# Two score maps of a differential attention head: from zero-padded 128-row operands to shared 64-row halves

## The reference

```
p1 = softmax(q1 @ k1.T * scale - slope * |t - s|)
p2 = softmax(q2 @ k2.T * scale - slope * |t - s|)
o  = (p1 - lam * p2) @ v        # then RMS norm over 128, gain
```

## Time and profile before

| what | value |
|---|---|
| median of 3 runs | 916.52 us |
| the runs | 917.79, 916.52, 912.07 us |
| span of the profiled execution | 912.4 us |
| busy in it: PE, PEld, DVE, ACT, POOL | 83%, 70%, 66%, 57%, 28% |

### The profile page before, as it was taken

One profiled execution on the slowest core, in us unless ns is written; L12 is line 12 of the kernel. 1 busy time (PEld: TensorE's weight loads), 2 busy tenths in 40 slices (PEclk: granted clock), 3 DMA queues, 4 the chain that ended last, 5 costly groups with the idle time before them and its releaser, 6 DMA issues. The chain is left out here.

```text
span 912.4 us, 13783 instructions
## 1 busy us (share of the span) xinstructions
PE 754.5 (83%) x4074; PEld 638.1 (70%) x4074; DVE 602.4 (66%) x1003; ACT 518.5 (57%) x960; POOL 257.5 (28%) x309
## 2 busy tenths in 40 slices
PE   3999999978887988779995249999999999999810
PEld 3998899867675766658884237888877777777600
DVE  6831210498885777731655954989988888888525
ACT  2252321778885888731125004878887787877412
POOL 5010000154453444320124461232123322232116
PEclk9999999989997999969995559999999999999965
DMA  8122110000002000039133722999999999999543
GB/s 301 62 57 82 49 55 1 1 21 2 1 1 92 1 2 0 1 93 372 69 137 117 253 93 60 362 389 365 388 391 388 378 377 388 391 389 381 184 156 143
DMA packets 70986, 159.50 MB, mean 175 GB/s; under 512 B 7457, under 2 KB 15649, under 8 KB 70945
## 3 DMA queue, kind: packets, MB, share of 16 engines
q1 hardware_dynamic: 66048, 141.16, 41.3%
q0 software_dynamic: 4896, 17.83, 7.6%
HBM read 139.57 MB, written 19.40 MB: 174 GB/s over the span
## 5 line engine op out<-in xcount | busy, mean ns | idle before, releaser
L1917 DVE TENSOR_TENSOR eDl<-rawD,eDh 128x1024 fp32r<-128x1024 f32 x64 | 75.4, 1219 | 14.0 <-ACT eDh L1861 13.8
L1917 DVE TENSOR_TENSOR eGl<-rawG,eGh 128x1024 fp32r<-128x1024 f32 x64 | 76.2, 1222 | 11.8 <-ACT eGh L1861 10.9
L1917 DVE TENSOR_TENSOR eUl<-rawU,eUh 128x1024 fp32r<-128x1024 f32 x64 | 75.0, 1221 | 4.9 <-ACT eUh L1861 4.3
L1976 POOL DMA_INDIRECT acc_rows<-yg,idx_s x17 | 27.3, 1605 | 157.8 <-ACT yg L1886 157.8
L1861 ACT ACTIVATE eGh<-rawG 128x1024 fp32r<-128x1024 f32 x64 | 66.1, 1057 | 5.8 <-DMA rawG<-in_w_gate 4.7
L1861 ACT ACTIVATE eUh<-rawU 128x1024 fp32r<-128x1024 f32 x64 | 63.5, 1053 | 7.2 <-DMA rawU<-in_w_up 7.2
L1809 PE MATMUL bank<-eGh,xgT_h 128*128 128x512 f32 x136 | 56.8, 418 | 12.4 <-DVE xgT_l L1922 11.8
L1861 ACT ACTIVATE eDh<-rawD 128x1024 fp32r<-128x1024 f32 x64 | 64.0, 1055 | 0.0
L480 DVE TENSOR_TENSOR w_l<-w_raw,w_h 128x1024 fp32r<-128x1024 f32 (+2 forms) x16 | 17.7, 1146 | 66.3 <-ACT w_h L379 66.3
L312 PE MATMUL bank<-w_h,xT_h 128*128 128x256 f32 (+1 forms) x192 | 55.1, 287 | 2.8 <-DVE xT_l L472 2.8
L1830 PE MATMUL bank<-eDh,hT_h 128*128 128x512 f32 x136 | 53.8, 395 | 2.2 <-DVE hT_l L1934 2.2
(11 more groups left out here) (325 smaller groups left out, 2366.8 us busy)
## 6 DMA issues: line engine op xcount, KB each, us to landing
rawG<-in_w_gate SPq DMA_DIRECT2D x68, 512.0 KB, 14.2
rawU<-in_w_up SPq DMA_DIRECT2D x68, 512.0 KB, 11.3
rawD<-in_w_down SPq DMA_DIRECT2D x68, 512.0 KB, 11.0
w_raw<-in_w_in SPq DMA_DIRECT2D x7, 1024.0 KB, 5.8
wo_raw<-in_w_o SPq DMA_DIRECT2D x16, 256.0 KB, 4.9
acc_rows<-ax SPq DMA_DIRECT2D x7, 512.0 KB, 2.6
x_rows<-res SPq DMA_DIRECT2D x6, 512.0 KB, 2.8
res<-acc_rows SPq DMA_DIRECT2D x6, 512.0 KB, 5.7
```

The costliest lines, as they stand in the source:

```text
L1917: nc.vector.tensor_tensor(wl_[X][i][:], raw_of(X, t, i)[:], f32(wh_[X][i][:]), ALU.subtract).then_inc(s_lo[X], 1)
L1976: pool.indirect_dma_start(out=acc_rows, out_offset=bass.IndirectOffsetOnAxis(ap=idx_s[:, 0:1], axis=0), in_=yg[:], in_offset=None, bounds_ ...
```

## The change

The queries of both maps go into one tile per sequence, laid out as the keys are. ACT and DVE cut them with one 128-partition instruction where there were two of 64. The zero rows, their memsets and their semaphore `s_zero` are gone. PE takes 64 partitions of q and k for each matmul: 0 to 63 for map 0 and 64 to 127 for map 1. The six matmuls of a tile now alternate between the maps, so that map 0's sum is complete after the fifth and map 1's after the sixth, where it was the third and the sixth. PE's wait for the two free banks of a tile is now one wait, for both, ahead of the first matmul. `s_qkh` counts 4 per head instead of 6, `s_ql` 2 instead of 4.

```diff
-    q_h = [[at(f"q_h{x}{m}", 78 + 6 * m + 4 * x, [P, SEQS[x][1]], FR) for m in range(2)] for x in range(2)]
-    q_l = [[at(f"q_l{x}{m}", 80 + 6 * m + 3 * x, [P, SEQS[x][1]], FR) for m in range(2)] for x in range(2)]
+    q_h = [at(f"q_h{x}", 78 + 4 * x, [P, SEQS[x][1]], FR) for x in range(2)]
+    q_l = [at(f"q_l{x}", 80 + 3 * x, [P, SEQS[x][1]], FR) for x in range(2)]
...
                 if qt == 0:
 
-                    wait(pe, s_zero, 2 * x + 2)
-                    wait(pe, s_ql, 4 * h + 2 * x + 2)
+                    wait(pe, s_ql, 2 * h + x + 1)
                     wait(pe, s_kl, 2 * h + x + 1)
-                for m in range(2):
-
-                    wait(pe, s_bias, 2 * g - 4 + m + 1)
-                    qs = slice(qt * P, (qt + 1) * P)
-                    out = psum[2 * (i % 2) + m][:, 0:n]
-                    nc.tensor.matmul(out, q_h[x][m][:, qs], kk_h[x][:], start=True, stop=False)
-                    nc.tensor.matmul(out, q_l[x][m][:, qs], kk_h[x][:], start=False, stop=False)
-                    nc.tensor.matmul(out, q_h[x][m][:, qs], kk_l[x][:], start=False, stop=True).then_inc(s_sc, 1)
+                wait(pe, s_bias, 2 * g - 4 + 2)
+                qs = slice(qt * P, (qt + 1) * P)
+                last = []
+                for k, (q, kk) in enumerate(((q_h, kk_h), (q_l, kk_h), (q_h, kk_l))):
+                    for m in range(2):
+                        r = slice(64 * m, 64 * m + 64)
+                        last.append(nc.tensor.matmul(psum[2 * (i % 2) + m][:, 0:n], q[x][r, qs], kk[x][r, :],
+                                                     start=(k == 0), stop=(k == 2)))
+                last[-2].then_inc(s_sc, 1)
+                last[-1].then_inc(s_sc, 1)
...
-                for m in range(2):
-                    r = slice(64 * m, 64 * m + 64)
-                    nc.scalar.activation(q_h[x][m][r, :], dqT[r, h, t0:t0 + n], ACT.Copy).then_inc(s_qkh, 1)
+                nc.scalar.activation(q_h[x][:], dqT[:, h, t0:t0 + n], ACT.Copy).then_inc(s_qkh, 1)
...
-            for x in range(2):
-                for m in range(2):
-                    r = slice(64 - 64 * m, 128 - 64 * m)
-                    nc.gpsimd.memset(f32(q_h[x][m][r, :]), 0.0)
-                    nc.gpsimd.memset(f32(q_l[x][m][r, :]), 0.0).then_inc(s_zero, 1)
...
-            pool.wait_ge(s_zero, 4)
             stage(0, 0)
...
-                for m in range(2):
-                    r = slice(64 * m, 64 * m + 64)
-                    wait(dve, s_qkh, 6 * h + 3 * x + m + 2)
-                    nc.vector.tensor_tensor(q_l[x][m][r, :], dqT[r, h, t0:t0 + n], f32(q_h[x][m][r, :]), ALU.subtract).then_inc(s_ql, 1)
+                wait(dve, s_qkh, 4 * h + 2 * x + 2)
+                nc.vector.tensor_tensor(q_l[x][:], dqT[:, h, t0:t0 + n], f32(q_h[x][:]), ALU.subtract).then_inc(s_ql, 1)
```

More of the change, by code:

```diff
@@ L585, in encoder_trunk @@
     s_alibi = sem("alibi_landed")
-    s_zero = sem("zero_rows_ready")
     s_qkh, s_ql, s_kl = sem("diff_qk_high"), sem("diff_q_low"), sem("diff_k_low")
@@ L906, in cut_q @@
                 t0, n, _ = SEQS[x]
-                for m in range(2):
-                    r = slice(64 * m, 64 * m + 64)
-                    wait(dve, s_qkh, 6 * h + 3 * x + m + 2)
-                    nc.vector.tensor_tensor(q_l[x][m][r, :], dqT[r, h, t0:t0 + n], f32(q_h[x][m][r, :]), ALU.subtract).then_inc(s_ql, 1)
+                wait(dve, s_qkh, 4 * h + 2 * x + 2)
+                nc.vector.tensor_tensor(q_l[x][:], dqT[:, h, t0:t0 + n], f32(q_h[x][:]), ALU.subtract).then_inc(s_ql, 1)
             def cut_k(h, x):
                 t0, n, _ = SEQS[x]
-                wait(dve, s_qkh, 6 * h + 3 * x + 1)
+                wait(dve, s_qkh, 4 * h + 2 * x + 1)
                 nc.vector.tensor_tensor(kk_l[x][:], dkT[:, h, t0:t0 + n], f32(kk_h[x][:]), ALU.subtract).then_inc(s_kl, 1)
```

## The result

The changed kernel takes **927.1 us** in the median of four runs (919.5 to 930.5), the kernel before 914.3 (908.3 to 917.8) on the same chip: a ratio of **1.0135, with a 95% interval of 1.0075 to 1.0195**. The forecast was 907.6 us; the time lies outside its range, on the other side of no change, and within 0.4 us of the 927.5 that one rival gave, the one in which the clock falls. I had given it 0.04. The intervals in this document are worked out from the runs that lie within 1.5% of the quickest of their kernel, which for every kernel but e10 are all of them.

A forecast was written before the change was run, and what follows sets the result against it. The differential block was taken as one chain along DVE, crossing to ACT at six waits, with PE slack. Savings 5.8 + 2.2 + 0.9 = 8.9 us from a 916.5 us median gave 907.6 us, range 903 to 914.5.

The forecast's parts named there:

- Parts 1 and 2: Cuts of q for heads 1 to 3: one instruction instead of two saves 5.8 us on DVE, 2.2 us through ACT.
- Part 3: Block start: first bias instruction comes sooner, gaining 0.9 us, between -0.2 (maps' matmuls in turn) and 1.8 (side by side).
- The sum: Whole change: cuts on DVE, cuts on ACT and block start, 5.8 + 2.2 + 0.9 = 8.9 us saved.
- Part 4: PE's score matmuls in the heads: 7 us or 3.5 us a head, both covered by PE's slack, so 0 gained.
- The rival of the clock: Differential block: less PE work brings more low-clock stretches; half the stage low costs +11 us, 927.5 us; chance 0.04.
- The array empties at each switch: PE's scores: each switch between halves makes a matmul cost 0.39 us, not 0.23; +10 us, 926.5 us; chance 0.07.
- The low ends: Cuts and start: POOL slows the surviving cut, ACT's relief becomes waits, start gains nothing; 4.1 us saved, 912.4 us; chance 0.22.
- Concurrent maps also shorten the heads: Scores in the heads: six matmuls take the time of three, saving 10.7 us in all, 905.8 us; chance 0.17.

The follow-up runs named there:

- e10: Changed kernel plus two 64-row filler matmuls (rows 0 to 63) ahead of each tile's scores; ten runs from 904.9 to 940.3 us, median 923.5.
- e2: Changed kernel, but each score matmul takes all 128 rows, so each bank sums both maps; 904.43 us, 0.9899 of the kernel before.
- e6: Changed kernel with three full-row score matmuls per tile instead of six on 64 rows, other products left out; 960.64 us, total not comparable (more expert tiles).
- e1: Changed kernel, but map 0's three 64-row score matmuls are issued before map 1's three; 924.35 us, 1.0119 of the kernel before.
- e5: Changed kernel, but both maps' score matmuls use rows 0 to 63, map 1's scores left out; 971.39 us, total not comparable (more expert tiles).
- e3: Changed kernel plus two full-row filler matmuls ahead of each tile's six scores, into banks the scores overwrite; 906.11 us, 0.9926 of the kernel before.
- e4: Kernel before with only the scores changed: 64 rows, alternating maps, one wait for both banks; 931.11 us, 1.0175 of the kernel before.
- e7: Changed kernel plus one full-row filler matmul ahead of each tile's six scores; 907.08 us, 0.9940 of the kernel before.
- e8: Changed kernel plus four full-row filler matmuls ahead of each tile's six scores; 915.73 us, 1.0014 of the kernel before.
- e9: Changed kernel plus full-row filler matmuls, one ahead of each long-sequence tile and four ahead of each short one; 901.67 us, 0.9869 of the kernel before.
- e12: Changed kernel plus four full-row filler matmuls ahead of each short-sequence tile, none ahead of long ones; 902.00 us, 0.9881 of the kernel before.

## Why the prediction was wrong

**Parts 1 and 2, the cuts, held.** In the changed kernel DVE cuts q once per sequence, in 0.69 and 0.42 us, so none of the surviving cuts inside the heads was slowed, though POOL's `second` runs beside each of them:

```profile
208.98 0.42 DVE L899 TENSOR_TENSOR q_l<-dqT,q_h 128x256 fp32r<-128x256 f32 x1
...
218.96 0.69 DVE L899 TENSOR_TENSOR q_l<-dqT,q_h 128x512 fp32r<-128x512 f32 x1
```

In e2, where PE does not disturb it, head 2 takes 19.62 us, head 1 18.92; the forecast said about 20.5. So these two heads gave 3.5 and 3.7 us instead of 2.6 each, and head 0 gave less (0.6), for a sum over the three of 7.8 us against the 8.0 of Parts 1 and 2.

**Part 3, the start, held in kind.** The scores of the two halves ran beside each other, the case that I had priced at 1.8 us:

```profile
183.07 0.83 DVE L899 TENSOR_TENSOR q_l<-dqT,q_h 128x512 fp32r<-128x512 f32 x1
...
185.78 0.69 DVE L926 CUSTOM_DVE_ANT_0 ee<-bank,bias_t 128x512 f32<-128x512 f32 x1 [0.32 <-PE bank L744]
```

The first bias instruction comes 1.6 us sooner than in the earlier trace rows. Beside the staging copies that moved to where the memsets were, the first cut of q takes 0.83 us and the key cut ahead of it 0.83 (0.69 before), the few tenths foreseen. In e2, whose maps run one after the other, the first bias instruction comes only 0.8 us sooner (186.59).

**The sum** of these was 8.9 us. e2 took 8.6 us off the median (904.43 against 912.99 on its chip), and its block ended 9.6 us sooner. The sum held, its terms less so: head 0 gave 2.0 us less than foreseen, heads 1 and 2 gave 2.0 more, and the last head, which has no cuts, gave 1.1 where none was forecast. In head 2 DVE's busy time fell by 2.3 us and its idle time by 1.5, where the forecast had 1.9 and 0.7. That 8.6 is so near 8.9 is in part luck.

**Part 4 is the step that failed**, in the words "so both values are covered by PE's slack: 0". I weighed two values for the scores, 7 us and 3.5 us a head, and both were counted at the high level. That the *kind* of matmul could set the level for everything else on PE was not among the terms. The concurrency itself came as the better case, 3.5 us of PE per head, and at the low level it was worth 0.7 (6.3 us of scores against 7).

**The rival of the clock had the right time from the wrong premise.** It said that the clock would fall where PE has too little to do, and "one costs nothing as long as DVE leads". By that premise 0.04 was fair, and e6 bears it out: half the score time on full rows left 0.85 and a block 7.2 us shorter than before. Two things were different. The low level held in a stretch in which PE was busy throughout, so it may well have fed itself: at 1.2 GHz PE leads, and a PE that leads did not win the clock back for 67 us here, more than 70 in e1 and 54 in e10. And half of the stage low had been the size assumed, 3 us a head; head 2 grew by 3.7, and from the fourth scaling of the bias table to the end of the block it was 44.2 us against 33.6. The rival's +11 us stood on a base of 916.5, the measured +12.8 on one of 914.3. The block came out at +11.1 because the first two heads were still ahead, and the clock was low for some 77 us of it, not for half. So that the time agrees within 0.4 us is luck.

The Trainium skill's page "TensorE: Matmul & The Clock Gate" (Part 1: The HAM clock gate) ties the low level to an idle engine and the high one to a busy engine. The trace agrees for the thin stretch at 192 us, and disagrees from 216 to 282 us and in e5, where PE is busy 84.00 of 84.00 us at 0.50. The measurement decides: busy time in the profile is not a sufficient sign of a high clock.

**The other rivals.** *The array empties at each switch*: the change of mode does cost time, some 0.20 us on entering and 0.16 on leaving at the high level (e3), but only at the two ends of a tile's scores, not at each of six matmuls; six tiles a head make some 2.2 us, which the 3.5 of the halved scores still pay for. The Trainium skill's page "TensorEngine Tiling (Array Packing)" (Key Properties) says that a change of mode drains the engine; the gaps agree with it. *The low ends*: not borne out, since the surviving cut takes 0.69 us beside POOL, and e2 shows the saving. *Concurrent maps also shorten the heads*: the overlap is there, and no kernel here shows its gain by itself, because each that had it at a high clock also had fillers.

**What is shown and what is not.** Shown: the scores alone bring the loss (e4); neither the order nor the double wait does (e2, e3); less PE work alone does not (e6); 64-row scores at full length hold the clock at 0.50 (e5); full-row work added to the mix brings it back (e3, e7, e8, e9), work of the same length on 64 rows does so only in some runs (e10). Argued, not shown: that it is the number of rows of a matmul that counts. In the changed kernel the two halves run together, so that all 128 rows are at work in every pair, and the clock stays low even so. Open: what the chip counts, and so how much full-row work is just enough; e12, with fillers in a third of the tiles only, has 0.86 in its block and is not measurably slower than e9. A clean price for concurrency at a steady high clock stays open too.

## What to carry to other kernels

Before splitting full-height matmuls into packed halves, ask what the rest of the engine's work costs at half the clock; if PE would then be the longest engine of the stage, halving a third of its work can lose. After such a change read the granted clock of the stage first, and beside it the busy share: here a low clock with PE full was a matter of what the array was given, not of gaps. If the clock has fallen, a few full-row matmuls that nobody needs, placed where PE has slack, are a cheap test and here a remedy (from 1.0135 of the time before to 0.9869).

## What the runs showed of the hardware

- Two 64-row matmuls of 512 columns on different halves of the rows start together and cost one step of 0.23 us at the high level and 0.42 at the low one, the step of one full-row matmul.
- They do so even when three matmuls of one half are issued ahead of the three of the other (e1), and 64-row fillers on rows 0 to 63 ran beside the scores of rows 64 to 127 (e10).
- On the same half they follow one another at the full step of 0.43 us at the low level (e5).
- Entering a group of 64-row matmuls costs about 0.20 us and leaving it about 0.16, at the high level (e3).
- With 64-row scores in the mix the clock stayed at 1.2 GHz for 66 us in which PE was busy throughout (the changed kernel) and for 84 us and more (e5); it came back with such scores still running at 266 us in e1 and at 250 us in e10.
